# A prologue reordered: weighing by arrival, rows scaled in place, and GpSimd's sums put behind the norm

## The reference

```python
cond = silu(c)                                   # c: one vector of 1024
mod = cond @ ada_w[0] + ada_b[0]                 # 6 x 1024
sh1, sc1, g1, sh2, sc2, g2 = split(mod, 6)
hn = (x * rsqrt(mean(x * x, -1) + eps) * norm1_g) * (1 + sc1) + sh1
u = hn @ w_in                                    # gate and x branch, 1024 channels each
xb = conv4(u_x) + b                              # along time
r, i = sigmoid(xb @ wa + ba), sigmoid(xb @ wx + bx)   # 8 heads of 128 x 128
log_a = -8 * r * softplus(-lam)
a, b = exp(log_a), sqrt(-expm1(2 * log_a)) * (i * xb)
y = scan(a, b) * gelu(u_gate)                    # h[t] = a[t] h[t-1] + b[t]
x = x + g1 * (y @ w_out)
...                                              # norm, top-2 mixture of 16 experts, final norm
```

## Time and profile before

| | us |
|---|---|
| runs, median (lowest to highest) | 1262.69 (1257.14 to 1269.31) |
| profiled execution, its own time | 1262.1 |
| its span | 1260.4 |
| TensorE busy | 1093.1 (87%) |
| VectorE, ScalarE, GpSimd busy | 768.6, 650.0, 611.9 |
| first x-branch matmul of channel 0 | starts 73.30 |
| first x-branch matmul of channel 1 | starts 143.64 |

### The profile page before, as it was taken

How to read it: one execution, slowest core, us unless ns; L and a number is a source line. 1 busy time by engine, 2 the same in 40 slices (tenths; PEclk the granted TensorE clock), 3 DMA queues, 4 the chain that set the end, 5 groups by cost and what they waited for, 6 DMA issues and landing times. The chain is left out here.

```text
span 1260.4 us, 18928 instructions
## 1 busy us (share of the span) xinstructions
PE 1093.1 (87%) x4857; PEld 850.4 (67%) x4858; DVE 768.6 (61%) x1198; ACT 650.0 (52%) x900; POOL 611.9 (49%) x665
## 2 busy tenths in 40 slices
PE   2797999999999997379999992599799999999991
PEld 2686788888888885368888871476466666766660
DVE  3477866667657664536677778356456655656541
ACT  3988766776677666322222212255556655555541
POOL 0061726637447340022567767146555655666553
PEclk9788999999999999689999995699999999999996
DMA  9550334433343312661445627857687887776751
GB/s 362 194 193 29 107 102 135 154 117 121 118 156 118 117 51 83 220 231 69 152 179 189 234 118 267 271 191 252 222 297 245 288 299 245 261 250 231 246 168 51
DMA packets 130871, 231.00 MB, mean 183 GB/s; under 512 B 24104, under 2 KB 91776, under 8 KB 129296
## 3 DMA queue, kind: packets, MB, share of 16 engines
q1 hardware_dynamic: 88976, 118.15, 28.2%
q0 software_dynamic: 23632, 62.49, 13.5%
q10 hardware_dynamic: 18224, 49.90, 11.6%
HBM read 175.87 MB, written 91.31 MB: 212 GB/s over the span
## 5 line engine op out<-in xcount | busy, mean ns | idle before, releaser
L1687 PE MATMUL po<-w_dn,e_ah 128*128 (+1 forms) x312 | 147.1, 616 | 16.9 <-issue 8.9
L1666 PE MATMUL pl<-w_hi,e_xh 128*128 (+1 forms) x312 | 140.9, 452 | 11.8 <-DVE e_xl L1577 6.3
L1210 PE MATMUL po<-wo_hi,b_yh 128*128 128x512 f32 x256 | 105.0, 410 | 28.0 <-DVE wo_lo L1024 28.0
L1668 PE MATMUL pl<-w_hi,e_xl 128*128 (+1 forms) x312 | 124.7, 400 | 0.0
L1667 PE MATMUL pl<-w_lo,e_xh 128*128 (+1 forms) x312 | 124.0, 397 | 0.0
L558 DVE SCALAR_TENSOR_TENSOR XB<-xu,v_cols,XB 128x512 f32<-128x512 f32 x96 | 90.1, 939 | 43.2 <-ACT XB L336 39.5
L1687 PEld LDWEIGHTS po<-w_dn,e_ah 128*128 128x128 f32 x312 | 57.9, 195 | 80.0 <-issue 80.0
L1377 POOL TENSOR_TENSOR e_ob<-e_obs,e_fg 128x1024 f32<-128x1024 f32 x38 | 91.1, 2397 | 32.2 <-ACT e_obs L1495 32.2
L674 PE MATMUL pg<-hT_hi,wg_hi 128*128 128x512 f32 x256 | 103.1, 403 | 0.0
L1211 PE MATMUL po<-wo_lo,b_yh 128*128 128x512 f32 x256 | 101.6, 397 | 0.0
L1212 PE MATMUL po<-wo_hi,b_yl 128*128 128x512 f32 x256 | 101.6, 397 | 0.0
(11 more groups left out here) (287 smaller groups left out, 2637.4 us busy)
## 6 DMA issues: line engine op xcount, KB each, us to landing
e_xg<-hn_slots ACTq DMA_DIRECT2D x40, 512.0 KB, 5.4
e_xa<-x_slots ACTq DMA_DIRECT2D x38, 512.0 KB, 3.8
stg<-in_ada_w_dram POOLq DMA_DIRECT2D x32, 512.0 KB, 4.2
w_raw<-in_moe_w_down_dram SPq DMA_DIRECT2D x16, 1024.0 KB, 7.3
w_raw<-in_moe_w_gate_dram SPq DMA_DIRECT2D x32, 384.0 KB, 4.3
w_raw<-in_moe_w_up_dram SPq DMA_DIRECT2D x32, 384.0 KB, 5.7
n_ada<-in_ada_w_dram ACTq DMA_DIRECT2D x4, 2048.0 KB, 18.4
hn_slots<-in_x_dram SPq DMA_DIRECT2D x16, 512.0 KB, 5.4
```

The lines of the kernel that those rows point to most:

```text
L1210: nc.tensor.matmul(po[u][:, hcols], yh[u][:, tok], wo_hi[:, k, hcols], start=(k == 0), stop=False)
L1666: nc.tensor.matmul(gu[:], xh[:, tok], hi, start=(k == 0), stop=False)
L1668: last = nc.tensor.matmul(gu[:], xl[:, tok], hi, start=False, stop=(k == KD - 1))
L1687: last = nc.tensor.matmul(dst, ah[:, k * P:(k + 1) * P], rows, start=(k == 0), stop=(k == KF - 1))
```

## The change

Seven edits, all in `norm_and_lru`:

- VectorE's `weigh` steps come right after their transfers: in pairs, with the small constants of the decay (`sp_t`) made between them.
- ScalarE's Abs, Exp and Ln for these constants move up behind `squares(0)`.
- From tile 5 on (`FIRST_SCALED`) VectorE scales the rows of the tile in place (128 x 1024) rather than a diagonal (128 x 128), and TensorE turns them with a plain transpose.
- `n_diag` has four buffers rather than two and lies over `macc`.
- TensorE sums `acc` after five turned tiles rather than ten, and only three more are turned ahead of the first projection; tiles 8 to 15 are turned between the products of channel 0.
- ScalarE and VectorE finish group 2 behind the first chunk's `gates_out` in channel 0's first half, next to group 3; four evacuations stand ahead of it.
- GpSimd's first block waits for the last `hT_lo` of group 3 (`lo_ready` at 32), and channel 0's `mod_sum` stands at the end of the channel.

```diff
-            for it in range(4):
+            squares(0)
+            act.wait_ge(vec_ready, 1)
+            nc.scalar.activation(sp_t[:, 0], lam, ACT.Abs).then_inc(s_a, 1)
+            ... Exp, then Ln behind s_b
+            for it in range(1, 4):
                 squares(it)
-            for it in range(4, 14):
-                evacuate(it - 4)
-                squares(it)
-            ...
+            evacuate(0)
+            squares(4)
+            evacuate(1)
+            convert("x", 0)
+            evacuate(2)
+            squares(5)
+            evacuate(3)
+            convert("g", 0)
+            act.wait_ge(gw_in, 32)
+            nc.scalar.activation(gwh[:], gw[:], ACT.Copy).then_inc(gw_hi_done, 1)
+            squares(6)
+            evacuate(4)
+            squares(7)
+            squares(8)
             finish_group(0)
-            for it in range(14, NT):
-                evacuate(it - 4)
+            for it in range(5, 8):
+                evacuate(it)
+            for it in range(9, 12):
                 squares(it)
             finish_group(1)
-            evacuate(12)
-            evacuate(13)
+            ...
+            evacuate(8)
+            evacuate(9)
+            squares(12)
+            squares(13)
+            squares(14)
...
-                if it >= 2:
-                    dve.wait_ge(turned, it - 1)
-                nc.vector.tensor_scalar(diag[:, it % 2], cst["ident"][:], rstd[:, it:it + 1], None, ALU.mult)\
-                    .then_inc(diag_ready, 1)
+                if it >= NDIAG:
+                    dve.wait_ge(turned, it - NDIAG + 1)
+                if it < FIRST_SCALED:
+                    ... the diagonal
+                else:
+                    nc.vector.tensor_scalar(xt[it % XR][:], xt[it % XR][:], rstd[:, it:it + 1], None, ALU.mult)\
+                        .then_inc(diag_ready, 1)
...
+            diagonal(2)
+            weigh(4)
+            weigh(5)
+            diagonal(3)
+            diagonal(4)
+            weigh(6)
+            weigh(7)
+            low_weights("x", 0)
+            diagonal(5)
+            low_weights("g", 0)
+            low_gates(0)
+            diagonal(6)
+            columns()
+            diagonal(7)
+            finish_group(0)
+            for it in range(8, 12):
+                diagonal(it)
+            finish_group(1)
+            diagonal(12)
+            diagonal(13)
+            diagonal(14)
...
             load(0, 0)
             load(0, 1)
+            pool.wait_ge(lo_ready, NT // 4 * KD)
...
-            for it in range(10):
+            for it in range(5):
                 turn(it)
             ... the sums of acc
-            turn(10)
-            turn(11)
+            for it in range(5, 8):
+                turn(it)
...
                         project("x", px[n], (h * NH + n) * NB, not at_least(j, 1)).then_inc(x_mm, 1)
                         if h == 0 and not at_least(j, 1):
-                            turn(12 + 2 * n)
-                            turn(13 + 2 * n)
+                            turn(8 + 2 * n)
+                            turn(9 + 2 * n)
                     if h == 1:
-                        if not at_least(j, 1):
+                        if at_least(j, 1):
+                            mod_sum()
+                        else:
                             pe.wait_ge(zT_ready, NT)
-                        mod_sum()
...
                         project("g", pg[n], (h * NH + n) * NB).then_inc(g_mm, 1)
+                        if h == 0 and n == 0 and not at_least(j, 1):
+                            for it in range(12, NT):
+                                turn(it)
                         gates(h, n)
+                if not at_least(j, 1):
+                    mod_sum()
```

More of the change, by code:

```diff
@@ L94, in norm_and_lru @@
         macc = sb("macc", [P, NB])
+        XT = ("A", "T", "M", "GE", "TI")
+        XR, NDIAG, FIRST_SCALED = len(XT), 4, 5
         acc = over("n_acc", [P, 2 * D], "stg")
-        vrow, diag = over("v_rows", [VROWS * KD, P], "mtmp"), over("n_diag", [P, 2, P], "XBh")
-        XT = ("A", "T", "M", "GE", "TI")
+        vrow, diag = over("v_rows", [VROWS * KD, P], "mtmp"), over("n_diag", [P, NDIAG, P], "macc")
         xt = [over("n_x_" + n, [P, D], n) for n in XT]
@@ L285, in _ @@
+            for it in range(9, 12):
                 squares(it)
             finish_group(1)
[L287 to L288 removed]
+            act.wait_ge(cond_ready, 1)
+            nc.scalar.activation(xu[:, 0, 0:CONV - 1], zero[:], ACT.Copy).then_inc(halo_ready, 1)
+            evacuate(8)
[3 more added lines that the diff above has]
+            squares(14)
             def gates_out(c, n, j):
@@ L373, in body @@
                     if begins and h == 0:
-                        evacuate(14)
-                        evacuate(15)
+                        evacuate(10)
+                        squares(15)
+                        evacuate(11)
                     if before:
@@ L499, in _ @@
             nc.vector.tensor_scalar(sp_t[:, 5], sp_t[:, 4], 0.0, None, ALU.is_equal).then_inc(s_b, 1)
+            diagonal(1)
+            weigh(3)
             dve.wait_ge(s_b, 3)
@@ L584, in body @@
                     low_xb(c, 0)
+                    if begins and h == 0:
+                        diagonal(15)
                     if before:
@@ L652, in turn @@
                 for k in range(KD):
-                    last = nc.tensor.matmul(pt[it % 2][:, k * P:(k + 1) * P], xt[it % XR][:, k * P:(k + 1) * P], diag[:, it % 2],
-                                            start=True, stop=True)
+                    rows, dst = xt[it % XR][:, k * P:(k + 1) * P], pt[it % 2][:, k * P:(k + 1) * P]
+                    if it < FIRST_SCALED:
+                        last = nc.tensor.matmul(dst, rows, diag[:, it % NDIAG], start=True, stop=True)
+                    else:
+                        last = nc.tensor.transpose(dst, rows, cst["ident"][:])
                 last.then_inc(turned, 1)
```

60 lines of the change are left out of this document (12 added, 48 removed).

## The result

The changed kernel took 1251.09 us (median of 20 runs, 1244.53 to 1255.75), the kernel before 1257.87 in the same sitting (20 runs, 1252.96 to 1271.27): a ratio of 0.9938 with a 95% interval of 0.9918 to 0.9958. So it is about 8 us faster, by the interval 5 to 10, inside the 1% that the prediction called no change. The profiled execution took 1252.2 (span 1250.5), against 1262.1 before and 1254 predicted.

What follows compares the result with a forecast made beforehand. TensorE is busy throughout each channel, so channel 1's start was taken to bound the kernel: forecast at 135.6 instead of 143.64, 8.0 us earlier, with GpSimd's block ending channel 0. Profiled 1262.1 less 8 gave 1254, range 1245 to 1262.

Steps and rivals of the forecast that it cites:

- Case A: The forecast itself: the wait for GpSimd's first block ends channel 0; 1254 us, chance 0.55.
- The prediction's other signs: Trace marks: group 2 starts near 92, not past 95; channel 1 starts near 135.6; its period stays 50.2 us.
- Part 1: Opening, weighing by arrival: weighing ends at 38.6, columns at 45.8, group 0 starts at 46.9; gain 20.8 us.
- the sums: TensorE behind the weighing: sums run from 38.6 to 45.4 us, at the old 6.8.
- part 3: ScalarE's squares and evacuations move behind group 0, giving 8 us back; group 3 ends at 107.2.
- case C: ScalarE's chain through the norm: TensorE's answers come 1 to 2 us late; gain 0 to 3, chance 0.17.
- Part 2: Rows scaled in place: cost VectorE about 0.5 us each, gain TensorE up to 1 a turn, neither decisive.
- The constants: ScalarE's decay constants in the opening: from 17.0 to 21.3 with two 1.28 us table loads; diagonal 1 waits.
- The gelu's wait: Channel 0's second half: TensorE finishes the x branch at 107.8 and waits 5 us for the first gelu.
- Part 4: Channel 0's second half: XBl at 120.5, last gates from 129.3 to 130.8 instead of 142.15 to 143.64.
- Part 5: GpSimd's first block takes 27.3 us from 107.2 to 134.5; waiting for it takes 4 to 5 us of the gain.
- The clock behind the gap: TensorE's 3.7 us gap ahead of channel 1 may cost the clock: 0 to 0.5 us set aside.

Runs made afterwards that it cites:

- second run: The changed kernel unaltered, run again beside the kernel before: 1252.46 us, ratio 0.9926.
- six edits: The changed kernel without GpSimd's part (no wait for the norm, channel 0's `mod_sum` between the second half's products as before): 1247.61 us, ratio 0.9925 to the kernel before.
- third run: The changed kernel unaltered, run once more beside the kernel before: 1248.89 us, ratio 0.9944.

## Why the prediction was right, and where its steps were off

**The end.** Predicted 1254 from a profiled 1262.1, a ratio of 0.9936; measured 0.9938. Case A happened: `mod_sum` stands still and GpSimd's last sum releases it. The prediction's other signs hold too: group 2 starts at 89.56, not past 95, and channel 2 takes 50.21 us (channel 1 takes 1.4 us more than before). That the ratio agrees so closely is luck: its interval is 0.4% wide, and the gain at the landmarks was 1 to 3 us larger than the forecast's 8, made of errors that partly cancel.

**Part 1, the opening: right but for the sums.** The weighing ended at 37.83 (38.6 predicted). The sums were costed at the 6.8 us of the earlier trace rows, which are from the 1.2 GHz level (the granted clock of that stretch is 0.50); TensorE had turned tiles without a break from 30.12 to 38.56, and they took 3.63. That term is 3.2 us too large (2.0 in the second run, where they took 4.84 behind 0.28 us of idle). Group 0 came only 2.2 earlier than forecast (44.67 for 46.9), because VectorE then waited 1.11 for ScalarE's root of tile 7; in the second run it came at 44.84, longer sums or not. The part's "20.8 us at the columns" is the gain at group 0's start; measured were 23.1 there and 24.2 at the columns. Everything behind runs 2 us ahead of the forecast: group 1 at 61.09 (63.0), group 2 at 89.56 (91.6), the last `hT_lo` at 105.03 (107.2). The hand-made chain of part 3 held step by step, which is what case C doubted.

**Part 2, scaling in place: size right, weight wrong.** The instruction takes 0.75 (0.8 predicted), a turn by transposes 1.03 to 1.07 at the full clock. But "neither decides alone", with at most 1 us gained a turn, was wrong: at the landmarks it is worth about 4 us, 3.7 at channel 1 and 4.2 at the output product against the first run of the kernel after. The step that failed is that the turns "run beside ScalarE's work". With diagonals ScalarE waits 1.8 longer for turn 7, which runs at the low clock behind the idle stretch of 6.14 or 8.31 us; it was priced from a full-clock row, where the earlier trace rows also held 2.53 behind an idle stretch. For turns 12 to 15 it waits 2.9 longer: each costs only 0.9 more, as the prediction has it, but ScalarE waits for every one of them. Less 0.5 that it then waits less for the first gates, that is the 4.2 by which group 2 comes later.

**The constants, without a price.** The prediction has them inside part 1 as a delay of diagonal 1, and as "one of four table loads" less. They delayed the weighing by nothing that shows (37.83, and 38.14 without them ahead of it). What the move itself is worth is not known: the kernel before had them in a stretch ahead of group 0 (36.65 to 64.3) in which ScalarE never waited, and no run puts them back there. The run with late constants shows that behind group 1 they would cost 5 to 6 us. Nor were the order of the weighing, the earlier sums and the place of group 2 tried one by one. The runs show what the six edits give together, and that about 4 us go when rows are no longer scaled in place.

**The gelu's wait** (part 4 of the prediction): 5 predicted, 4.65 measured.

**Part 4, the last gates: hardly earlier than forecast.** `XBl` came at 118.46 (120.5 predicted), and the last gates began at 127.83 (129.3), but they ended at 130.3, where 130.8 was said. TensorE had stood for 2.19 us and fell to the low clock from 128.4 on (0.63 each): six matmuls took 2.5 for 1.5.

**Part 5, GpSimd's block: a good price, a wait of half the size.** 26.65 for 27.3 predicted, begun 2 us earlier, so it ended at 131.9 for 134.5. The wait forecast was 3.7; the block ended 2.6 us sooner and the gates half a microsecond sooner, which leaves the 1.64. The prediction said that it takes 4 to 5 us of the gain, in exchange for an undisturbed norm. The runs put both sides into numbers: without the wait the norm ends 3.0 to 4.0 later and channel 1 begins 2.1 to 3.3 earlier. The Trainium skill's rule ("SBUF — State Buffer", "Who interferes with whom"), by which one of VectorE and GpSimd holds the shared ports until it is done, agrees in direction: each slows the other. Here the block took 22.3 us beside norm groups 0 and 1 and 26.65 beside taps and scan.

**The clock behind the gap.** 0 to 0.5 us were set aside. The first three x matmuls of channel 1 took 2.07 from start to start (133.05 to 135.12). In the run without a wait, where `mod_sum` stands at the same place and the clock is full, they took 1.10, so about 1.0 us went there; twice the term. In the third run of the same kernel, with a wait of 1.20 in place of 1.64, they took 1.10 too; its channel 1 started 0.3 earlier and its output product 1.0.

**The sum.** Channel 1 was forecast at 135.6 and came at 133.05. Of the 2.6 us between, 1.9 are the earlier norm (the sums, less VectorE's wait) and 0.65 GpSimd's block. So the gain at that landmark was 10.6 for 8.0 (9.7 and 10.9 in the other two profiled runs), and 9.4 at the output product (8.6 and 10.3), behind the microsecond of the clock. In the run without a wait channel 1 takes 51.59 us as well, of which 0.73 is a new wait ahead of its first gates (at 155.18). The forecast was 1 to 3 us short at the landmarks, which is less than the whole times can show.

## What to carry to other kernels

Small work costs nothing in an engine's early waits and more than its duration in a full stretch: there it brings its table loads and waits along (5 to 6 us here for three activations of 0.2). Before calling such a move a gain, look where the kernel before had the work. Before moving an engine that shares memory ports with the critical one, ask for each place whom it slows, and whether its end now has a waiter; contention that only changes place gains nothing. And when the tail of a kernel varies by more than the change is worth, read the start of the next stage in the trace, not the median alone; and run the median all the same, since it can hold what the landmark does not show.

## What the runs showed of the hardware

- The sums of 32 passes with one column each took 6.83 us at a granted clock of 0.50 (1.2 GHz) and 3.63 at 1.00 (2.4 GHz): products with a single column follow the clock by nearly a factor of two.
- Behind idle stretches of 2.19 and 4.65 us TensorE's first matmul still took 0.51 and 0.47, and from the third on they took 0.63: a fast first matmul does not show that the gap was free. It need not go so: behind the same 2.19 us the first took 0.79 in the third run of this kernel, and behind 2.03 us in the run with diagonals only all six stayed at the full clock.
- The same `TENSOR_SCALAR` of 128 x 512 on GpSimd took between 0.69 and 4.77 us:

```profile
110.03 0.69 POOL L646 TENSOR_SCALAR mtmp<-stg,cond 128x512 f32<-128x512 f32 x1
...
119.79 2.48 POOL L646 TENSOR_SCALAR mtmp<-stg,cond 128x512 f32<-128x512 f32 x1 [0.17 <-POOL macc L648]
...
134.22 4.77 POOL L642 TENSOR_SCALAR macc<-stg,cond 128x512 f32<-128x512 f32 x1 [1.25 <-PE n_pt L716]
```

The first ran beside an idle VectorE, the second beside its scan. During the third, VectorE issued four instructions with two inputs each, back to back; the first and the last of them:

```profile
134.68 1.20 DVE L471 TENSOR_TENSOR wg_lo<-raw_g,wg_hi 128x1024 fp32r<-128x1024 f32 x1
...
137.29 1.21 DVE L548 SCALAR_TENSOR_TENSOR T<-M,T 128x1024 f32<-128x1024 f32 x1
```

They took the 1.20 and 1.21 of an undisturbed VectorE, and GpSimd was done at 138.99, half a microsecond behind the last of them. It looks as if GpSimd waited out the whole series; the trace does not show who held what. Beside the taps both engines were slowed.
